# A DiT step with a mixture of experts on one core: the order of the pieces of an attention head, and where the conditioning products stand among them

## What is computed

```python
def finish_layer(x, o_mla, o_conv, o_na, gate1, shift2, scale2, gate2, lp):
    mix = jnp.concatenate([o_mla, o_conv, o_na], axis=-1)
    x = x + gate1 * jnp.dot(mix, lp['w_out'])
    h = rms_norm(x, lp['norm2_g']) * (1 + scale2) + shift2
    return x + gate2 * grouped_moe(h, ...)

def modulation(cond, w_ada, b_ada):
    return jnp.split(jnp.dot(jax.nn.silu(cond), w_ada) + b_ada, 6, axis=-1)
```

## Time and profile before

| | us |
|---|---|
| median of 3 runs (lowest, highest) | 1148.38 (1147.41, 1151.89) |
| the profiled execution | 1147.22 |
| its span | 1145.4 |
| TensorE busy | 1085.2 (95%) |
| VectorE busy | 881.7 (77%) |
| ScalarE busy | 701.5 (61%) |
| GpSimd busy | 228.2 (20%) |

### The profile page before, as it was taken

One profiled execution on the slowest core, in us unless ns is written; L12 is line 12 of the kernel. 1 busy time (PEld: TensorE's weight loads), 2 busy tenths in 40 slices (PEclk: granted clock), 3 DMA queues, 4 the chain that ended last, 5 costly groups with the idle time before them and its releaser, 6 DMA issues.

```text
span 1145.4 us, 14964 instructions
## 1 busy us (share of the span) xinstructions
PE 1085.2 (95%) x5668; PEld 864.1 (75%) x5668; DVE 881.7 (77%) x1077; ACT 701.5 (61%) x921; POOL 228.2 (20%) x213
## 2 busy tenths in 40 slices
PE   5899899999899999999999999889899999999996
PEld 2677556688778888888878877678878888888884
DVE  1368555674699999899975888865679999899894
ACT  2334265543487788888855357661278788887880
POOL 2201312011232221222101042211205121221100
PEclk9999899998999999999999998979899999999998
DMA  9866688845589999999952332113599999999971
GB/s 379 337 259 265 239 340 309 324 186 202 234 334 359 370 382 390 366 388 383 397 237 60 129 126 64 48 66 139 207 342 370 357 389 381 369 373 376 373 294 56
DMA packets 54298, 320.66 MB, mean 280 GB/s; under 512 B 11626, under 2 KB 11738, under 8 KB 19280
## 3 DMA queue, kind: packets, MB, share of 16 engines
q1 hardware_dynamic: 38448, 276.59, 62.6%
q0 software_dynamic: 15776, 43.08, 10.1%
HBM read 313.40 MB, written 25.44 MB: 296 GB/s over the span
## 4 chain that ended last, share of the span: by engine, by line
PE 75%; DVE 14%; DMA 3%; ACT 3%; issue 2%; POOL 1%; SPq 0%; DVEq 0%; POOLq 0%; ACTq 0%
PE bank L1272 40%; PE bank L901 6%; DVE w_lo L2427 5%; PE bank L1172 5%; PE bank L919 4%; PE bank L884 3%; DMA ring<-wring_dram 3%; PE bank L1031 3%; PE bank L962 2%; PE bank L996 2%; PE bank L1264 2%; PE bank L891 2%; PE bank L1208 1%; PE bank L929 1%; PE bank L1345 1%
## 5 line engine op out<-in xcount | busy, mean ns | idle before, releaser
L2427 DVE TENSOR_TENSOR w_lo<-ring,w_hi 128x2048 fp32r<-128x2048 f32 x192 | 436.4, 2288 | 42.7 <-ACT w_hi L1703 42.6
L1703 ACT CAST w_hi<-ring 128x2048 fp32r<-128x2048 f32 x192 | 367.2, 1917 | 35.2 <-PE bank L1272 34.8
L1272 PE MATMUL bank<-w_hi,hgT_hi 128*128 128x512 f32 x512 | 203.9, 398 | 6.5 <-issue 4.6
L1272 PE MATMUL bank<-w_hi,hgT_lo 128*128 128x512 f32 x512 | 200.9, 392 | 0.0
L1272 PE MATMUL bank<-w_lo,hgT_hi 128*128 128x512 f32 x512 | 200.8, 392 | 0.0
L812 POOL DMA_INDIRECT y_rows<-y,y_at x26 | 48.2, 1854 | 352.8 <-ACT y L1734 332.5
L1272 PEld LDWEIGHTS bank<-w_hi,hgT_hi 128*128 128x128 f32 x512 | 96.9, 189 | 27.4 <-issue 8.1
L1272 PEld LDWEIGHTS bank<-w_hi,hgT_lo 128*128 128x128 f32 x512 | 96.9, 189 | 20.5
L1272 PEld LDWEIGHTS bank<-w_lo,hgT_hi 128*128 128x128 f32 x512 | 97.1, 190 | 19.3
L1272 PE MATMUL bank<-w_hi,hidT_hi 128*128 128x512 f32 x256 | 102.3, 400 | 0.0
L1272 PE MATMUL bank<-w_hi,hidT_lo 128*128 128x512 f32 x256 | 100.2, 391 | 0.0
(11 more groups left out here) (303 smaller groups left out, 1817.8 us busy)
## 6 DMA issues: line engine op xcount, KB each, us to landing
ring<-wring_dram SPq DMA_DIRECT2D x258, 1024.0 KB, 8.2
y_rows<-hg POOLq DMA_DIRECT2D x6, 1024.0 KB, 6.2
kT<-mod_dram POOLq DMA_DIRECT2D x4, 1024.0 KB, 8.6
late<-y_rows POOLq DMA_DIRECT2D x4, 1024.0 KB, 14.6
ring<-wring_dram SPq DMA_DIRECT2D x4, 832.0 KB, 10.4
h_rows<-h_tok POOLq DMA_DIRECT2D x6, 512.0 KB, 2.9
ring<-wring_dram SPq DMA_DIRECT2D x4, 640.0 KB, 10.7
bias<-na_bias_dram POOLq DMA_DIRECT2D x32, 64.0 KB, 6.6
```

Of the source, the lines that this page charges most:

```text
L1272: mm = pe.matmul(b[:, :], a, w[m], start=(start and k == 0), stop=(stop and k == 2))
L1703: act.copy(w_hi[:, q, :], in_ring(l, expert_slot(e, i))).then_inc(hi_made[q], 1)
L2427: dve.tensor_tensor(w_lo[:, q, :], in_ring(l, expert_slot(e, i)), w_hi[:, q, :], ALU.subtract) \
```

## The change

In each round the pair of layer 0 comes right behind the head's scores (on TensorE, and on ScalarE its copies come first in the round), the values of head i-2 come ahead of the turn of head i-1, and ScalarE copies the turned probabilities of i-1 ahead of the exponentials of i. `psum_plan` is changed alike, so the banks of most pieces move. VectorE, GpSimd and SyncE keep their programs but for the banks.

```diff
--- before.py
+++ after.py
@@ -219,12 +219,15 @@
     for i in range(len(GROUPS) + 2):
         if i < len(GROUPS):
             order += [("S", i, t) for t in range(3)]
+
+        pairs(pairs_after(n, "turn", i))
         if i == 0:
             order += [("q", 1, t) for t in range(3)] + [("kv", 1, t) for t in range(4)]
+
+        if i >= 2:
+            order += [("O", i - 2)]
         if 1 <= i <= len(GROUPS):
             order += [("PT", i - 1, 0), ("PT", i - 1, 1)]
-        if i >= 2:
-            order += [("O", i - 2)]
         if i == len(GROUPS):
             order += [("mix", t) for t in range(TILES)]
         if i == 3:
@@ -235,7 +238,6 @@
             order += [("cb", t) for t in range(3)]
         if i == 11:
             order += [("ln", 0), ("ln", 1)]
-        pairs(pairs_after(n, "turn", i))
     order += [("turn", p) for p in open_group]
     order += [("out", 0, 0), ("mix", 3), ("mix", 4), ("out", 1, 0), ("shift",)]
     for t in range(1, TILES):
@@ -1117,13 +1119,14 @@
                 for i in range(len(GROUPS) + 2):
                     if i < len(GROUPS):
                         scores(l, i)
+                    modulation(l, pairs_after(n, "turn", i))
                     if i == 0:
                         queries(l, 1)
                         keys_values(l, 1)
+                    if i >= 2:
+                        values(l, i - 2)
                     if 1 <= i <= len(GROUPS):
                         turn_probs(l, i - 1)
-                    if i >= 2:
-                        values(l, i - 2)
                     if i == len(GROUPS):
 
                         pe.wait_ge(*once_read(l, ("O", 7)))
@@ -1151,7 +1154,6 @@
                         pe.wait_ge(*once_read(l, ("cb", 2)))
                         for c in range(2):
                             turn_around(l, ("ln", c), [ln_tm[:, t, c * P:(c + 1) * P] for t in range(TILES)])
-                    modulation(l, pairs_after(n, "turn", i))
                 close_modulation(l)
 
                 def out_product(t, p, lo, hi):
@@ -1663,13 +1665,15 @@
                 evac_modulation(l, pairs_after(n, "heads"))
                 evac_turned(l, 0)
                 for i in range(len(GROUPS) + 2):
+                    evac_modulation(l, pairs_after(n, "turn", i))
+                    if 1 <= i <= len(GROUPS):
+
+                        evac_probs(l, i - 1)
                     if i < len(GROUPS):
                         exponentials(l, i)
                     if i == 0:
                         evac_heads(l, 1)
                         square_keys(l, 1)
-                    if 1 <= i <= len(GROUPS):
-                        evac_probs(l, i - 1)
                     if i == 4:
                         square_neighbours(l)
                     if i == 3:
@@ -1691,7 +1695,6 @@
                     if i == len(GROUPS):
                         for t in range(1, TILES):
                             mix_high(l, t)
-                    evac_modulation(l, pairs_after(n, "turn", i))
                 close_modulation(l)
                 for i in range(TILES, TILES + 2):
                     mix_high(l, i)
```

## The result

The changed kernel took a median of 1167.7 us (1166.7 to 1173.1, 4 runs) against 1149.4 us for the kernel before, run beside it (1147.4 to 1151.9, 4 runs): a ratio of **1.0147**, 95% interval 1.0105 to 1.0189. The profiled execution took 1168.1 us with a span of 1166.3 (before: 1147.2 and 1145.4).

What follows compares the result with a forecast made beforehand. TensorE was taken as the bound, with 75% of the chain. Layer 0's +0.8 - 2.2 + 1.3 + 0.9 + 0.6 + 1.6 = +3.0 and layer 1's 0 gave 1151.4 us on the median's scale, range 1144 to 1158.

Steps and rivals of the forecast that it cites:

- The loop: Next head's scores wait for exponentials to free banks: layer 0 6.5 us a bound head for 5.84, layer 1 4.0 for 3.85.
- list of signs: Expected in the changed profile, such as layer 0 exponentials about 5 us after scores began and 6.5 us between heads.
- Head 4: Layer 0: scores of head 4 start 1.4 us earlier, or 2.2 earlier without the ring's 0.8.
- The ring: Head 0, layer 0: the moved pair waits for its second half's slot, between 0 and 1.7 us, taken as 0.8.
- Head 8 and the end of layer 0: Scores of head 8 +0.8 us; head 10's exponentials at 226.0 for 222.99; then ScalarE's same work to the table load.
- +3.0 for layer 0: Layer 0's net loss up to the table load for the swish, which starts about 234.1 us.
- rival B: Loop plus one or two low-clock stretches at new thin places (head 7, both layers), 3.4 and 1.7 us: 1156.5; chance 0.3.
- +0 of layer 1: Layer 1: no net change, table load at 763.3 for 763.24 us; -5.5 were the clock full after a shorter wait.

Runs made afterwards that it cites:

- after_mended: Changed kernel with the turn of head 11 back ahead of the values of head 10 and four waits filled with idle products; 1153.7 us, ratio 1.0029.
- last_turn: Changed kernel with only the turn of head 11's probabilities back ahead of the values of head 10, in both layers; 1165.1 us, ratio 1.0134.
- filled: Changed kernel with idle products at the turn of layer 1's last four heads and ahead of head 11's scores in layer 0; 1162.5 us, ratio 1.0107.
- before_o8: Kernel before with the layer 1 values of head 8 and turned probabilities of head 10 in other banks; 1148.8 us, ratio 1.0017.
- before_sized: Kernel before with idle products sized to its waits, at one place in layer 0 and two in layer 1; 1141.9 us, ratio 0.9939.
- only_copies: Kernel before with one part of the change, ScalarE's copies of the turned probabilities ahead of the exponentials; 1159.3 us, ratio 1.0072.
- minus_values: Changed kernel with the turn of the probabilities put back ahead of the values; 1163.3 us, ratio 1.0054.
- minus_pairs: Changed kernel with the w_ada pairs put back at the end of the round; 1158.5 us, ratio 1.0054.
- only_values: Kernel before with one part of the change, values ahead of the turn of the probabilities; 1159.5 us, ratio 1.0099.
- banks: Changed kernel with its order kept and PSUM banks from head 1 to head 9 dealt by which was left first; 1160.6 us, ratio 1.0089.

## Why the prediction was wrong

**The loop: right in its mechanism, its terms too small.** "6.5 us" a head is 7.07. By its own terms, from start to start in the timeline: score 1 starts 1.34 us after the turn's end (191.45 - 190.11) for 1.1, scores 1 and 2 take 1.49 for 1.3, the pair 1.86 for 1.85, the values 1.61 for 1.51, the turn 0.77 as given. Of the 1.34 us, 0.73 are ahead of the exponential, for 0.5. ScalarE's second copy starts 0.36 us behind the turn's end, and a copy's length alone had been counted. The exponential of head 5 began 7.8 us after its scores (183.03 to 190.84), where the list of signs had "about 5 us" and its own sum gives 7.0. It also bound in the scores of head 3, and in layer 1 at 4.4 us a head (731.8 to 736.2 in after_mended) for 4.0. That no part alone closes it was not said in the prediction; the three kernels with two parts show it.

**Head 4: the number right, in part by luck.** -1.4 was given, -1.3 measured. But the 0.8 us of ring wait in it was 0.1, so that -2.2 had been due, and the loop's wait of 0.96 us in the scores of head 3 and the 3.4 us of low clock that went had not been counted. **The ring: right in place, too narrow.** Head 0 to 1 took 0.1 to 4.6 us more over the kernels with moved pairs; the longest wait was 2.79 us, past the bound of 1.7, and two kernels had 3.4 us of low clock with it.

**Head 8 and the end of layer 0: the step that failed.** Head 8 was given +0.8 and got +2.8: from -1.3, three heads each 1.23 us longer, and 0.4 more at the turn. What lies behind head 7's exponentials took 3.96 us (206.00 to 209.96), where the rows of before give 3.94 (6.78 less 2.84) and the prediction had counted 4.2, so all of the delay had come in with them. From head 8 to head 10's exponentials 2.2 us more had been given, and 3.4 were measured. For the rest the prediction said "From there to the end ScalarE sets the pace with the same work as before (8.1 us from 222.99 to 231.07)". It took 13.1 us (232.03 to 245.14). Two things had been left out. The clock fell behind a wait of 1.37 us at head 11, where no pair stands ahead of the scores any more; filling it gave 3.3 us. And the values of head 10 now stand ahead of the turn of head 11, whose copies are the last thing ScalarE does before the table load. At full clock the last_turn edit is worth some 0.7 us: the table load comes 1.3 us earlier in after_mended than in filled (30.6 for 31.9 us), but 0.6 of that is there already at the values of head 9, by fewer idle products. The +3.0 for layer 0 was +11.2.

**The clock: rival B was the case, and was too small.** B had the mechanism and one of the two places, the turn of the last heads in layer 1; in layer 0 it named head 7, where the clock stayed up, and not the end of the stage. Its price, 3.4 and 1.7 us, came from the two shorter low stretches in the head stages of the trace of before; the stretches were 10.2 and 25.0 us. The +0 of layer 1 was +6.0. The 13.7 us stretch in the earlier trace rows was in the trace and would have been the nearer row for "behind a wait in the head stage". The Trainium skill, "TensorE: Matmul & The Clock Gate", section "Part 1: The HAM clock gate", says that the throttled state is the default and activity releases it. The trace agrees with the first half: filling the waits kept the clock at 1.00. With the second it does not sit easily: from 758 to 762 us TensorE was busy 4.00 of 4.00 us at 0.50, and in before_o8 it was busy 18.00 of 18.00 us at 0.50 from 737 to 755.

**The sum.** Without the start the difference of the two profiled executions is 18.1 us. Some 8 of it came back by filling waits with the order unchanged (filled, by stretches), and about 14 of 17 by ratio with the last turn as well (after_mended); but part of the 14 is clock that the kernel before loses too. Like for like, after_mended against before_sized, the order itself costs 11.8 us: the loop 4.1, the end of layer 0 3.8 (1.6 from head 9 to 10, 1.4 from 10 to 11, 0.8 behind), the rest the ring wait with its low clock, which was next to nothing in the changed kernel's own profile.

**Open.** Why the clock falls behind waits of 1.44 and 0.43 us (before_o8) or 1.44 and 0.96 (only_copies) and not behind 1.44 and 0.76 (before), and why it then stays low for 3.4 us in one kernel (minus_values) and for 34 and 37.5 in these two, was not settled. A long wait is not always there either: in minus_pairs 6.8 us of low clock begin at 207.9 us, where the last wait above 0.3 us had ended 8 us before. It is open too why the five kernels with values ahead of the turn, the old banks and no filling had 24 to 26 us of it behind head 8 of layer 1, while without that part it was 13.7 to 35.5 us. The cost of values ahead of the turn in rounds before the last, seen in the 4.1 us from head 8 to the table load in only_values, was not split further. The prices of low clock rest on single profiled executions; the totals of ten executions bear out the fills of the kernel before, and those of the changed kernel only together with the last turn.

## What to carry to other kernels

When an in-order engine's piece is moved behind a wait, follow the chain until it comes back to the same engine, bank numbers included: three moves of which no two made a loop in layer 0 closed one together (in layer 1, without pairs, two were enough), and another dealing of the banks opened it again. A wait on TensorE can cost more than its length, by the clock that is lost behind it. Look for the waits ahead of each low stretch of the granted clock, and fill them with idle products no longer than the wait; here that made the kernel before 0.6% faster, where the reordering made it 1.5% slower. Compare two orders only when both are filled: a reordering that seems to cost 0.3% against the unfilled kernel (after_mended) costs 1% against the filled one. Time a filler once before counting with it (0.22 us a product here, where 0.12 had been reckoned).

## What the runs showed of the hardware

With waits of 0.95 and 1.61 us, 3.5 us apart, or one of 1.37 us, the granted clock fell from 1.00 to 0.50 in the changed kernel, and it held there when they were filled (filled, after_mended), where a wait of 3.09 us had been the visible case before. It then stayed at 0.50 for 10 us and more: in before_o8 for 37.5 us, of which TensorE was busy without a gap from 737 to 773 us. In only_copies a wait of 1.13 us falls into its 34 us. The first rise of the clock came at 22.1 us in the profiled execution of the kernel before and at 34.4 us in banks, with the same work up to there; with 3.4 us more of low clock shortly behind the rise, the products from 50 to 120 us came 5.6 us later.
